# A two-model transformer chain on one core: the first model's mix reordered, its output weights in units of 512 rows

## The reference, cut to what matters

```python
def token_mix(h, cos, sin, w_in, sgu_w, sgu_b, w_out):
    p = h @ w_in
    u = gelu(p[..., OFF_SGU_U:OFF_SGU_V]); va = gelu(p[..., OFF_SGU_V:OFF_Q])
    a_out = chunked_sgu(u, va, sgu_w, sgu_b)      # u * (causal w_s @ va + b_s), 4 groups, chunks of 128
    q, k, v = ...                                 # 8 heads of 64, rope on q and k
    qi, ki, wi = ...                              # index: 4 heads, one key head, weights per query
    b_out = dsa_attention(q, k, v, qi, ki, wi)    # softmax over the 64 best keys of each query
    return jnp.concatenate([a_out, b_out], axis=-1) @ w_out
x = x + g2 * token_mix(modulate(rms_norm(x, norm_mix), sh2, sc2), ...)
```

## Time and profile before

| | |
|---|---|
| median of 3 runs | 2208.77 us (2208.63 to 2212.23) |
| profiled execution | 2204.33 us, its span 2201.9 us |
| mean granted clock of TensorE | 0.980 |
| matmuls, weight loads | 15091 each |
| HBM read | 414 MB, 189 GB/s over the span |
| first mix | about 278 to 410 us of the span |
| second mix | about 818 to 950 us |

### The profile page before, as it was taken

One profiled execution on the slowest core, in us unless ns is written; L12 is line 12 of the kernel. 1 busy time (PEld: TensorE's weight loads), 2 busy tenths in 40 slices (PEclk: granted clock), 3 DMA queues, 4 the chain that ended last, 5 costly groups with the idle time before them and its releaser, 6 DMA issues.

```text
span 2201.9 us, 35839 instructions
## 1 busy us (share of the span) xinstructions
PE 2113.7 (96%) x15091; PEld 1949.4 (89%) x15091; DVE 1691.0 (77%) x2325; ACT 991.9 (45%) x1332; POOL 83.9 (4%) x68
## 2 busy tenths in 40 slices
PE   7998999999999999899999899999999999999998
PEld 7998887999999998799998678878878887889998
DVE  5899967888889886788887774787776568987563
ACT  3443444543444444453445564422323348764442
POOL 0100100100000010010010000000000001110000
PEclk8999998999999999899999999999999999999999
DMA  7898942799979975367774002254565232143652
GB/s 265 293 333 299 305 142 96 238 310 327 303 256 325 322 226 171 110 208 258 241 250 156 20 3 76 77 189 155 169 214 191 77 115 70 49 132 128 217 193 76
DMA packets 343111, 417.46 MB, mean 190 GB/s; under 512 B 13754, under 2 KB 267688, under 8 KB 342952
## 3 DMA queue, kind: packets, MB, share of 16 engines
q1 hardware_dynamic: 339840, 411.86, 56.5%
q10 hardware_dynamic: 3112, 3.33, 0.5%
HBM read 414.09 MB, written 1.05 MB: 189 GB/s over the span
## 4 chain that ended last, share of the span: by engine, by line
PE 42%; DVE 9%; ACT 4%; issue 2%; POOL 0%; DVEq 0%; ACTq 0%; POOLq 0%
PE pb L657 41%; DVE ACC L2184 2%; ACT wh L1517 1%; DVE wl L2176 1%; PE pb L1345 1%; DVE T L2184 1%; DVE SM L2771 1%; DVE RS L2266 0%; DVE Hl L2184 0%; DVE L_y L2184 0%; DVE T L2176 0%; DVE L_y L2176 0%; ACT L_y L1518 0%; DVE L_y L2892 0%; DVE L_u L2184 0%
## 5 line engine op out<-in xcount | busy, mean ns | idle before, releaser
L657 PE MATMUL pb<-Hh,wh 128*128 128x256 f32 (+1 forms) x2624 | 792.1, 302 | 27.1 <-DVE wl L2176 17.9
L657 PE MATMUL pb<-Hl,wh 128*128 128x256 f32 (+1 forms) x2624 | 777.9, 297 | 0.0
L657 PE MATMUL pb<-Hh,wl 128*128 128x256 f32 (+1 forms) x2624 | 774.0, 297 | 0.0
L2176 DVE TENSOR_TENSOR wl<-raw,wh 128x2048 fp32r<-128x2048 f32 (+3 forms) x271 | 602.0, 2225 | 176.1 <-ACT wh L1517 175.6
L1517 ACT ACTIVATE wh<-raw 128x2048 fp32r<-128x2048 f32 (+3 forms) x271 | 502.5, 1856 | 379.8 <-PE pb L657 202.5
L657 PEld LDWEIGHTS pb<-Hh,wh 128*128 128x128 f32 x2624 | 503.8, 192 | 48.3 <-DVE wl L2176 20.4
L657 PEld LDWEIGHTS pb<-Hl,wh 128*128 128x128 f32 x2624 | 503.9, 192 | 15.0 <-issue 1.9
L657 PEld LDWEIGHTS pb<-Hh,wl 128*128 128x128 f32 x2624 | 501.4, 192 | 12.8
L657 PE MATMUL pb<-Bh,wh 128*128 128x256 f32 (+1 forms) x1376 | 417.5, 303 | 11.2 <-DVE Y L2176 3.6
L657 PE MATMUL pb<-Bh,wl 128*128 128x256 f32 (+1 forms) x1376 | 414.0, 301 | 0.0
L657 PE MATMUL pb<-Bl,wh 128*128 128x256 f32 (+1 forms) x1376 | 414.0, 301 | 0.0
(11 more groups left out here) (261 smaller groups left out, 2113.5 us busy)
## 6 DMA issues: line engine op xcount, KB each, us to landing
raw<-in_ffn_w_in_dram SPq DMA_DIRECT2D x88, 1024.0 KB, 7.3
raw<-in_ada_w_dram SPq DMA_DIRECT2D x320, 256.0 KB, 4.0
raw<-in_mlp_w_dram SPq DMA_DIRECT2D x64, 1024.0 KB, 5.3
raw<-in_ada_w_dram SPq DMA_DIRECT2D x80, 512.0 KB, 5.0
raw<-in_ffn_w_out_dram SPq DMA_DIRECT2D x32, 1024.0 KB, 7.5
raw<-in_mix_w_in_dram SPq DMA_DIRECT2D x22, 1024.0 KB, 5.5
raw<-in_ffn_w_out_dram SPq DMA_DIRECT2D x16, 768.0 KB, 6.3
raw<-in_attn_w_qkv_dram SPq DMA_DIRECT2D x12, 1024.0 KB, 7.4
```

The costliest lines, as they stand in the source:

```text
L657: return e.matmul(o, l, r, start=st, stop=sp, skip_group_check=True)
L2176: return e.tensor_tensor(o, a, b, f)
```

## The change

In both mixes of the first model:

- `wi` goes to bank 0 in place of 6; the four filler matmuls before the second `u` unit of the second layer go. The logits run between the two halves of the second `u` unit, the two row halves into two banks and without TensorE's wait on itself; ACT's relus come before its split for the second `q` unit and the second gelu; DVE runs three parts of the search at once before its split for the first `k` unit, and the search ends before the last `va` unit.
- `sg` has four banks and stands before the last `v` unit; the gate's ada columns (`(0, l, 5)`) are due and flushed there, all finished columns of bank 7 are copied to `MOD`, and bank 7 is then free. DVE gates all four groups and ACT makes their `Bh` before the steps.
- The output weights become four units of 512 rows by 512 columns: `ma` (gated rows) twice, `mb` (attention rows) twice. The `ma` products run as four groups of 24 matmuls (256 columns each) in bank 7 behind steps 2, 4, 7 and 10, each added to `XC` by DVE; `mb` follows as before `mo`, the first one k-tile outermost. The splits of `ma` and `mb` on ACT and DVE stand between the steps.
- `ROOM` moves from `mo` (0.5 each) to `u` and `va` (0.5 each).

```diff
-ROOM = {"iq": 0.0, "ik": 0.0, "u": 0.0, "q": 0.0, "k": 0.0, "va": 0.0, "v": 0.0, "mo": 0.5, "fo": 0.8, "k2": 0.0, "v2": 0.0, "q2": 0.0, "o2": 0.0, "lr": 0.0, "lw": 0.0, "lo": 0.0, "lg": 0.0}
+ROOM = {"iq": 0.0, "ik": 0.0, "u": 0.5, "q": 0.0, "k": 0.0, "va": 0.5, "v": 0.0, "ma": 0.0, "mb": 0.0, "fo": 0.8, "k2": 0.0, "v2": 0.0, "q2": 0.0, "o2": 0.0, "lr": 0.0, "lw": 0.0, "lo": 0.0, "lg": 0.0}
@@ plan
                 for key, off in (("u", 0), ("q", OQ), ("k", OK), ("va", 512), ("v", OV)):
+                    if key == "v":
+                        need((0, l, 5))
                     for j in range(2):
                         cols(w, key, off + 256 * j)
-                need((0, l, 5))
                 for j in range(4):
-                    cols(t["mix_w_out"][l], "mo", 256 * j)
+                    cols(t["mix_w_out"][l], "mb" if j // 2 else "ma", 512 * (j % 2), nk=4, k0=4 * (j // 2), nc=512)
@@ RING
-        "rp": (0, 1), "rot": (2, 3), "wi": (6,), "lq": (4, 5), "vv": (0, 1), "mu": (6,), "mv": (4, 5), "sg": (4, 5), "mo": (4, 5),
+        "rp": (0, 1), "rot": (2, 3), "wi": (0,), "lq": (4, 5), "vv": (0, 1), "mu": (6,), "mv": (4, 5), "sg": (4, 5, 2, 3), "mo": (4, 5),
@@ build
+        GATED_AT = (2, 4, 7, 10)
@@ TensorE, mix
-                if l:
-                    stay(4, 4)
-                fm("u", "mu", h_at, 256, need)
-
-                def logits(b):
-                    nk = 128 * (b + 1)
+
+                def logits():
                     E.wait_ge("rope.q", q0 + 2)
-                    for g in range(2):
-                        p = fill("lq")
-                        for hh in range(2):
-                            r = slice(64 * hh, 64 * hh + 64)
-                            if hh:
-                                E.wait_ge("pe.step", E.n["pe.step"])
-                            ins = mm(p[:, 256 * hh:256 * hh + nk], M_iq[r, g, 128 * b:128 * b + 128], M_ik[r, 0:nk], True, True)
-                            if hh == 0:
-                                E.step(ins)
-                        full(ins, "lq")
-
-                logits(0)
-                logits(1)
+                    for b in range(2):
+                        nk = 128 * (b + 1)
+                        ps = [fill("lq") for _ in range(2)]
+                        for g in range(2):
+                            for hh in range(2):
+                                r = slice(64 * hh, 64 * hh + 64)
+                                ins = mm(ps[hh][:, 256 * g:256 * g + nk], M_iq[r, g, 128 * b:128 * b + 128], M_ik[r, 0:nk], True, True)
+                                if g:
+                                    full(ins, "lq")
+
+                fm("u", "mu", h_at, 256, need, behind={0: (logits,)})
...
-                tm("v", "vv", 2, h0)
                 E.up("rope.q", 6)
...
                     full(ins, "sg")
+                mods((0, 0, l, 5))
+                tm("v", "vv", 2, h0)
+                columns_out()
...
+                def gated(g):
+                    if g % 2 == 0:
+                        ma[:] = weights("ma")[:2]
+                    if g == 0:
+                        E.wait_ge("mod", E.n["mod"])
+                    E.up("mo.full")
+                    p = bank(7, "x", 2)
+                    for m in range(2):
+                        c = slice(128 * (2 * (g % 2) + m), 128 * (2 * (g % 2) + m) + 128)
+                        for kt in range(4):
+                            E.wait_ge("mo.in", in0 + kt + 1)
+                            ins = mm3(p[:, 256 * m:256 * m + 256], (ma[0][:, kt, c], ma[1][:, kt, c]), hid_at(0)(kt, 256), kt == 0, kt == 3)
+                    full(ins, "mo")
+
                 for n in range(STEPS1 + 3):
...
+                    if n in GATED_AT:
+                        gated(GATED_AT.index(n))
                 ob0 = E.up("ob.read", 2)
-                mods((0, 0, l, 5))
...
+                for m in range(2):
+                    fm("mb", "mo", lambda kt, n: hid_at(0)(kt + 4, n), 256, lambda kt: E.wait_ge("ob.read", ob0), fresh=m == 0, said="x", by=2)
@@ ACT, mix
                 gelu_u(0)
-                ahead("u")
-                gelu_u(1)
                 half_free(1)
...
+                ahead("u")
+                gelu_u(1)
                 ahead("q")
...
+                act(SM[:, 25:26], EPSC, ACT.Exp)
...
+                for g in range(4):
+                    E.wait_ge("mo.gate", 4 * l + g + 1)
+                    act(Bh[0][:, 256 * g:256 * g + 256], M_u[:, g, :], ACT.Copy).then_inc(sems["mo.hi"], 1)
...
+                    if n == 1:
+                        ahead("v")
+                    if n == GATED_AT[1] + 1:
+                        ahead("ma")
...
-                for m in range(4):
-                    ahead("mo")
-                    if m:
-                        squares(2 * m - 2)
+                ahead("ma")
+                E.up("x", 8)
+                ahead("mb")
+                squares(0)
+                squares(2)
+                squares(4)
+                ahead("mb")
                 squares(6)
@@ DVE, mix
                 ahead("u")
+                ix = itertools.chain(index(0), index(1))
+                for _ in range(3):
+                    next(ix)
                 ahead("q")
-                ix = itertools.chain(index(0), index(1))
                 next(ix)
...
+                for g in range(4):
+                    E.mark(tt(M_u[:, g, :], M_u[:, g, :], M_g[:, g, :], ALU.mult), "mo.gate")
+                g2 = mod(0, 0, l, 5)
+                ahead("v")
+                copy_columns()
...
+                    if n == 3:
+                        ahead("v")
+                    if n == GATED_AT[1] + 2:
+                        ahead("ma")
+                    for g in {0: (0, 1), 1: (2, 3)}.get(n, ()):
...
+                    if n - 1 in GATED_AT[:3]:
+                        added(GATED_AT.index(n - 1))
...
+                ahead("ma")
+                added(3)
+                for m in range(4, 8):
+                    added(m)
+                    if m % 2:
+                        ahead("mb")
```

More of the change, by code:

```diff
@@ L695, in mods, with columns_out @@
                 E.up("mod", len(keys))
+            def columns_out():
+                ranges = []
+                for c0 in sorted(c0 for key, c0 in columns if key not in COLS_DONE and c0 not in copied):
+                    copied.add(c0)
+                    if ranges and ranges[-1][1] == c0:
+                        ranges[-1][1] = c0 + 4
+                    else:
+                        ranges.append([c0, c0 + 4])
+                EARLY.append((flushed[0], ranges))
+                E.up("mod", len(ranges))
             def weights(key, low=True):
@@ L738, in fm @@
                             full(ins, kind)
+                        for f in behind.get(m, ()):
+                            f()
                 spent()
@@ L2255, in mod, with copy_columns @@
                 return MOD[:, c:c + 8]
+            def copy_columns():
+                cols, ranges = EARLY.pop(0)
+                E.wait_ge("cols", cols)
+                for a, b in ranges:
+                    E.mark(e.tensor_copy(MOD[:, a:b], PB[7][:, a:b]), "mod")
+                    early.update(range(a, b, 4))
+                E.wait_ge("mod", E.n["mod"])
             def gain(o, b, v, l, s, g):
@@ L2757, in _ @@
             gate_of(S_OC, 2, 0, 2, 1)
-            E.wait_ge("cols", EARLY["cols"])
-            for a, b in EARLY["ranges"]:
-                E.mark(e.tensor_copy(MOD[:, a:b], PB[7][:, a:b]), "mod")
-                early.update(range(a, b, 4))
+            copy_columns()
             p0, ob0 = E.n["p"], E.n["ob.read"]
```

70 lines of the change are left out of this document (23 added, 47 removed), and 2 rows, old and new, of the table GROUPS.

## The result

The changed kernel takes 2223.8 us (median of six runs, 2222.1 to 2226.0) against 2207.7 for the kernel before: ratio 1.0075, 95% interval 1.006 to 1.009. It is slower by 16 us. The profiled execution took 2224.0 us, its span is 2222.3, 20.4 over that of the profiled execution of before.

A forecast was written before the change was run, and what follows sets the result against it. TensorE, busy 96%, was taken to bound the kernel, with DVE's queue delaying it before the attention. 3.6 + 1.6 + 3.0 + 3.3 + 2.0 = +13.5 us moved the 2208.8 median to 2222.3; range 2205 to 2232.

The forecast's parts named there:

- the likeliest case: Whole kernel: the prediction's own forecast of 2222 us, slower by 13.5 us, chance 0.50.
- DVE before the attention: Before the attention: DVE's queue of search, splits and ada pieces delays TensorE; attention starts 3.6 and 1.6 us later.
- The early part's own gain: Up to the attention: without new waits, removed waits would let the attention start 6.3 and 5.6 us earlier.
- Waits in the attention: Between the attention's steps: new waits of 0.55, 1.8, 1.9, 1.9 and 1.1 us, so interleaving ends no sooner.
- (a): Attention step 3: DVE's split and the first add into XC hold bank 7, TensorE waits 1.8 us.
- (b): Attention step 5: ScalarE's split stands before the copy that frees bank 4, divisors wait 1.9 us.
- (c): Attention step 6: DVE's split delays M_ON, values 4 wait 1.9 us.
- the four Bh copies: Attention's start: ScalarE makes them before the first exponentials, so score 2 waits until 3.0 us from the start.
- The fold: Before the sum of squares: POOL's five adds end late and TensorE waits, +3.0 and +3.3 us.
- The clock in the attention: Attention: TensorE left at full clock, with no loss counted there.
- the third rival: Attention falls to half clock as today: 5 to 6 us more per mix, 2233 us, chance 0.12.
- the faster case: DVE no bound before the attention, which starts 6.3 and 5.6 us earlier: -5.6 us, 2203, chance 0.16.

The follow-up runs named there:

- e_pieces: e_early with only the room for ada pieces moved from mo to u and va (0.5 each): 2207.5 us.
- e_q: Changed kernel with the room for ada pieces moved from u and va to q (1.0), under the two u units: 2217.9 us.
- e_es: e_early with DVE's search parts cut as in the kernel before, the second q unit's split first: 2187.8 us.
- e_swap: Changed kernel with DVE's split in attention step 3 moved behind the first add into XC: 2216.3 us.
- e_late: Changed kernel with the first mb unit's split moved from attention steps 5 and 6 to steps 8 and 9: 2214.5 us.
- e_noil: Changed kernel with the four gated products behind the attention's steps in two mo banks, DVE's mb and second ma splits also behind: 2219.2 us.
- e_early: Kernel before plus only wi in bank 0, early logits, relus and search, and sg in four banks; ada pieces, output weights, attention as before: 2194.8 us.
- e_best2: Changed kernel with pieces at q, second q split between relus, and the e_late and e_swap edits; first u split still ahead of the rotation's product: 2190.7 us.
- e_mid: e_early with ScalarE's split of the second q unit between the relus of the first and second row tile: 2191.4 us.

## Why the prediction was right, and where not

The time (2222 forecast, 2223.8 measured) and the likeliest case were right. Counted to the end of the last v unit and from there to the sum of squares, the forecast was +4.6 and +2.6 us (the 1.0 each for the clock included), then +3.0 and +3.3; measured were +5.9 and +0.9, then +4.7 and +4.3: +13.5 in all against +15.8. The terms:

- **DVE before the attention: right.** Forecast waits in the first mix 0.25, 2.2, 3.4 and 3.9 at the k and va units, measured 0.47, 1.80, 3.31 and 2.06 (the last is shorter because TensorE came later to it, at a clock of 0.84 from 338.8 to 349.2, which is 1.7 us); in the second 0.3, 2.3, 3.6 and 0.9, measured 0.47, 0.94, 3.31 and 0.52; the piece at iq 1.2 more at the u unit, measured 1.42 for 0.22. The end of the last v unit is 1.3 us later than forecast in the first mix and 1.7 earlier in the second, so the size per mix was met less well than the sum. e_pieces and e_q show the cause by adding and removing it.
- **The early part's own gain: right in size.** Counted as an attention 6.3 and 5.6 us earlier without waits; alone it started 2.7 and 3.3 us earlier, with waits behind DVE's splits of 3.1 and 2.3 us left ahead of it. In e_es, where these waits are gone, it started 6.9 and 7.6 earlier.
- **Waits in the attention: right in place and nearly in size** (0.52, 1.82, 1.64, 1.33, 1.14 for forecast 0.55, 1.8, 1.9, 1.9, 1.1). The causes (a) and (b) are shown by e_swap and e_late, where the wait goes with the split; the last, the third add, fits e_noil, where no add stands between the steps and the wait is back at 0.35. Two causes were wrong. (c), DVE's split in front of M_ON: without that split the wait was 1.55, and the early part, which has no such split, has it too, as the kernel before had (1.54 at 379.40). That it belongs to the division itself is what is left, and not tested. And the four Bh copies ahead of the exponentials cost nothing that shows: score 2 starts 2.5 us after the first score with them and 2.5 in e_early without them (374.01 against 371.52, 362.86 against 360.34).
- **The fold: wrong.** The step that failed is "The sum begins at 50.9, not 47.9", a wait of TensorE for POOL. There was none, which the prediction itself had named as a sign of being wrong. POOL did end when forecast, but by two errors that cancel: the first squares came at 44.9 us and not at 41.8 (behind the last v unit's end at 371.0), and the five additions took 6.14 us and not the 9.3 of the earlier trace rows, so the end was at 51.1 for a forecast 51. TensorE, forecast there at 48.5, came only at 52.6. In e_best2, where TensorE is faster, POOL's five end at 401.1 and the sum begins at 402.65. So the terms of 3.0 and 3.3 us were not there.
- **The clock in the attention: wrong.** The step that failed is "I leave the attention at full clock". At the windows' granted clock, 5.0 of 38.4 us were lost to it. TensorE's 48.5 us of the forecast plus this would be 53.5; measured were 52.6 and 51.9. Only the third rival (chance 0.12) had such a term, and it happens to be nearly as large as the fold's: two errors of about 3 to 5 us per mix in opposite directions. That the sum was met is in this part luck.

Of the rivals, the faster case (DVE no bound) describes the early part without the pieces. The condition named for it, splits landing less than a microsecond late, is what e_mid fulfils, and it is faster by 0.7%.

In the mixes' times the loss divides into -10.0 us (e_early against before), +11.5 (e_pieces against e_early) and +14.2 (after against e_pieces: gated products and output weights in the attention), of which 12.9 stand from the attention on. Of these, e_late recovers 6.1 and e_swap 5.5, the clock's share included. In the first mix's attention the waits add up to 4.4 us more than in e_pieces, and by the granted clock (0.87 of 38.4 us against 0.92 of 22.0) about 3 us more are lost: an estimate that, less the flush of 0.8, comes near the measured 6.4.

Open: which of the better versions is best. The intervals of e_es, e_mid, e_early and e_best2 overlap, and the first block varies by more than they differ; by the mixes' own times it is e_mid. The two together, the old cut of the search and the split between the relus, were not tried. That products between the steps can beat products behind them is neither shown nor excluded: 90.5 us against 91.5 for both attentions of e_best2 and e_mid, or 90.7 without e_mid's flush, with the granted clock moving by more.

## What to carry to other kernels

When TensorE is busy 96% of the time, a helper engine's queue decides what a rearrangement brings: list what stands in it before each product that TensorE needs, and put background work (here the ada pieces) where that engine idles, not where the planner has room by the count of units. An interleaving that fills gaps brings its own splits and additions into the same queue; place these behind what the next matmul waits for. Test the parts of a compound change alone: here one part was worth -0.5%, and another, five pieces of background work moved to another place in the queue, took it all.

## What was not expected of the hardware

- POOL's additions of 128x256 took 1.2 us each (five in 6.14) where they stood beside less DVE work, DVE busy 10.2 of 14.4 us (the second row, the changed kernel), and 1.8 to 2.8 beside more splits: in e_early (the first row) one took 2.81 and four 7.17, DVE busy for 20.2 of 22.8 us. That DVE's work slows them was not tested by itself, and the DMA share differs in the same rows, 0.46 against 0.91.

```profile
382.00:404.75 22.75, 22.75 (x194) 22.75 (x192) 20.19 (x22) 10.40 (x14) 9.55 (x5) 1.00 0.91 300
...
409.20:423.60 14.40, 14.03 (x117) 13.88 (x116) 10.18 (x13) 8.67 (x12) 5.57 (x5) 1.00 0.46 146
```

- The granted clock in the same attention code was 1.00 in one mix and 0.84 in the other of one execution (e_early), 3.5 us and 0.5 us better than before. Waits of 1.1 to 1.9 us were followed by some 3 to 13 us at half clock in many places (behind product 1's wait after, where without the wait, in e_swap, the product ran at full clock), but not in all: the second mix of e_best2 went through its waits of 1.15, 1.55 and 1.13 us at 1.00. The runs give no rule for when the clock falls.

```profile
891.31:929.00 37.69, 33.39 (x279) 27.61 (x280) 24.77 (x60) 21.36 (x56) 0.47 (x1) 1.00 0.31 102
```
